# Summing the expert results in the output tensor, pass by pass, instead of gathering them at the end

## The reference: what is computed

```python
h = rmsnorm(x, odd_norm_ffn[i])
x = x + moe_swiglu(h, moe_w_router[i], moe_w_gate[i], moe_w_up[i], moe_w_down[i])

logits = xf @ w_router                       # 8 experts
top_logit, top_idx = lax.top_k(logits, 2)    # two experts for each token
gates = softmax(top_logit)
...
yb = lax.map(expert_block, (xb, block_e))    # swiglu of the rows of one expert
out = zeros.at[slot_tok].add(yb * slot_gate[:, None])
```

## Time and profile before

| | |
|---|---|
| median of three runs | 1993.7 us (1992.94 to 1994.46) |
| the profiled execution | 1992.27 us |
| its span, first to last instruction | 1990.4 us |
| PE busy | 1939.7 us (97%) |
| DVE busy / ACT busy / POOL busy | 734.7 / 651.3 / 496.7 us |
| mean DMA rate | 204 GB/s |
| mean granted clock of PE | 0.995 |

### The profile page before, as it was taken

The page is one execution under the profiler, slowest core; times in us unless marked ns, Lnnn a source line. Parts: engine busy times, 40 slices in busy tenths (PEclk is TensorE's granted clock), DMA queues, the critical chain, the costliest instruction groups (busy, mean ns, idle before and its releaser), DMA issues.

```text
span 1990.4 us, 28733 instructions
## 1 busy us (share of the span) xinstructions
PE 1939.7 (97%) x11839; PEld 1705.1 (86%) x11839; DVE 734.7 (37%) x1076; ACT 651.3 (33%) x1069; POOL 496.7 (25%) x263
## 2 busy tenths in 40 slices
PE   7999999999999999999899999999999999999996
PEld 7887778888888887877679999999999999888885
DVE  4725564210010005856632000010000101999996
ACT  4333322232222224356630000000000001888783
POOL 3546664265445543442121000000000000000010
PEclk9999999999999999999999999999999999999998
DMA  7962222233233332320009877878888787999995
GB/s 242 314 212 64 64 81 88 75 117 95 99 102 94 97 102 70 111 85 22 33 1 371 298 254 281 291 281 315 283 309 289 285 310 274 384 379 384 367 413 212
DMA packets 295103, 405.38 MB, mean 204 GB/s; under 512 B 11272, under 2 KB 211034, under 8 KB 294970
## 3 DMA queue, kind: packets, MB, share of 16 engines
q1 hardware_dynamic: 292666, 395.12, 56.9%
q0 software_dynamic: 2304, 8.39, 1.1%
HBM read 372.67 MB, written 30.80 MB: 203 GB/s over the span
## 4 chain that ended last, share of the span: by engine, by line
PE 92%; DVE 3%; POOL 2%; ACT 1%; issue 1%; DVEq 1%; SPq 0%; DMA 0%; POOLq 0%; ACTq 0%
PE ps L2000 21%; PE ps L2007 10%; PE ps L399 6%; PE ps L400 6%; PE ps L401 6%; PE ps L2061 5%; PE ps L2063 5%; PE ps L2062 5%; PE ps L417 3%; PE ps L419 3%; PE ps L418 3%; PE ps L547 2%; PE ps L549 2%; PE ps L548 2%; PE ps L436 1%; PE ps L435 1%
## 5 line engine op out<-in xcount | busy, mean ns | idle before, releaser
L1242 POOL TENSOR_TENSOR w_lo<-raw,w_hi 128x1024 fp32r<-128x1024 f32 (+1 forms) x159 | 387.9, 2448 | 353.8 <-ACT w_hi L935 353.6
L1847 DVE TENSOR_TENSOR s_lo<-s_raw,s_hi 128x1024 fp32r<-128x1024 f32 x198 | 235.4, 1222 | 22.0 <-ACT s_hi L2207 13.6
L2449 DVE TENSOR_TENSOR hid<-ps,silu_g 128x160 f32<-128x160 f32 x110 | 35.7, 324 | 543.0 <-ACT silu_g L2182 543.0
L935 ACT ACTIVATE w_hi<-raw 128x1024 fp32r<-128x1024 f32 (+1 forms) x159 | 164.8, 1043 | 192.2 <-PE ps L419 115.8
L399 PE MATMUL ps<-act_a_hi,w_hi 128*128 128x512 f32 x568 | 226.4, 399 | 0.0
L2182 ACT ACTIVATE silu_g<-ps 128x160 f32<-128x160 f32 x110 | 33.4, 304 | 585.9 <-PE ps L2000 585.9
L2000 PE MATMUL ps<-xT,w_up 128*128 128x132 f32 (+1 forms) x1760 | 224.2, 281 | 0.0
L2000 PE MATMUL ps<-xT,w_gate 128*128 128x132 f32 (+1 forms) x1760 | 224.2, 281 | 0.0
L400 PE MATMUL ps<-act_a_lo,w_hi 128*128 128x512 f32 x568 | 221.2, 390 | 0.0
L401 PE MATMUL ps<-act_a_hi,w_lo 128*128 128x512 f32 x568 | 221.2, 390 | 0.0
L2207 ACT ACTIVATE s_hi<-s_raw 128x1024 fp32r<-128x1024 f32 x198 | 205.6, 1059 | 42.6 <-PE ps L2063 37.3
(11 more groups left out here) (369 smaller groups left out, 2908.9 us busy)
## 6 DMA issues: line engine op xcount, KB each, us to landing
w_gate<-in_moe_w_gate SPq DMA_DIRECT2D x55, 1024.0 KB, 5.2
w_up<-in_moe_w_up SPq DMA_DIRECT2D x55, 1024.0 KB, 7.6
w_down<-in_moe_w_down SPq DMA_DIRECT2D x55, 1024.0 KB, 10.2
s_raw<-in_moe_w_gate SPq DMA_DIRECT2D x33, 1024.0 KB, 7.7
s_raw<-in_moe_w_up SPq DMA_DIRECT2D x33, 1024.0 KB, 7.6
s_raw<-in_moe_w_down SPq DMA_DIRECT2D x33, 1024.0 KB, 7.7
raw<-in_even_w_in SPq DMA_DIRECT2D x43, 512.0 KB, 5.2
raw<-in_attn_w_qkv SPq DMA_DIRECT2D x24, 512.0 KB, 3.7
```

The lines of the kernel that those rows point to most:

```text
L935: act.activation(w_hi[:, u % HL_SLOTS, 0:size(u)], raw[:, u % RAW_SLOTS, 0:size(u)], ACT.Copy).then_inc(hi_done, 1)
L1242: pool.tensor_tensor(w_lo[:, u % HL_SLOTS, 0:size(u)], raw[:, u % RAW_SLOTS, 0:size(u)], flat(w_hi[:, u % HL_SLOTS, 0:size(u)]), ALU.subtr ...
L1847: return eng.tensor_tensor(s_lo[u % S_HL][:], s_raw[u // 2 % S_RAW][:, u % 2, :], s_hi[u % S_HL][:].bitcast(F32), ALU.subtract)
```

## The change

The tensor `y_dram`, its zeros, the gathers and the last sums go. In their place:

- After the tile loads of round 6 of the first pass, SP stores the residual `x_sb` to `out`. From then on two of its tiles are free as `xp` and `xp2`.
- DVE computes, while the first pass begins, where each token stands in each expert's list (`tab_at`) and its token number with the gate (`tab_src`). POOL writes these pairs of 8 bytes with 32 indirect DMAs of 128 entries into a DRAM tensor `table`, sorted by pass, and SP reads it back as `tab` and `tab2` in the last round of the first pass.
- For each pass POOL fetches the rows of `out` that belong to its tokens by an indirect DMA into `xp` (and `xp2` for rows beyond 128), DVE computes `y_rows = PSUM * gate + xp` where ACT copied before, and POOL scatters `y_rows` back to `out`. Each fetch waits for the scatters of the pass before.
- In the first small pass DVE takes over the sums of the last wide pass, right behind the products of chunks 0 and 1; in the others both halves of `small_rows` are DVE's.
- After the last small pass no fetch, sum or store is left but the pass's own. The body of the extra passes (not run here) is longer.

```diff
-        zero_blocks = [(rows, r) for r in range(0, y_dram.shape[0], P) for rows in (y_dram, h_slots)]
+        zero_blocks = list(range(0, h_slots.shape[0], P))
...
@@ SP
-                if r == 1 and t >= 1:
-                    store_small_rows(t - 1)
-                if r == 2 and t == 0:
-                    store_rows(WIDE - 1)
...
-                if r == 5 and w >= 1:
-                    store_rows(w - 1)
+                if r == 6 and w == 0:
+                    sp.wait_ge(acc_evac, 44 + NT)
+                    for tt in range(NT):
+                        sp.dma_start(out[0, tt * P:(tt + 1) * P, :], x_sb[:, tt, :]).then_inc(out_stored, 16)
+                if r == ROUNDS - 1 and w == 0:
+                    by_pass = table.rearrange("(w c) a -> c w a", w=E)
+                    sp.wait_ge(scattered, 16 * 2 * NT + 16 * NT * E)
+                    sp.dma_start(tab[:], by_pass[0:P, :, :]).then_inc(tab_in, 16)
+                    sp.dma_start(tab2[0:CAP2, :, :], by_pass[P:CAP, 0:WIDE, :]).then_inc(tab_in, 16)
         for t in range(SMALL):
             load_small(t)
-        store_small_rows(SMALL - 1)
...
-        for tt in range(NT):
-            sp.wait_ge(out_made, tt + 1)
-            sp.dma_start(out[0, tt * P:(tt + 1) * P, :], x_sb[:, tt, :]).then_inc(out_stored, 16)
         sp.wait_ge(out_stored, 16 * NT)
@@ ACT
-                if r == 0 and t >= 1:
-                    small_y_copy(t - 1, 0)
...
-                if t == 0 and r == 0:
-                    act.wait_ge(y_turned, 2 * WIDE - 1)
-                    act.wait_ge(y_stored, 32 * (WIDE - 1))
-                    copy_y(y_rows, P)
...
-                if f == 4 and w >= 1:
...
-                    copy_y(y_rows, P)
@@ POOL
+        pool.wait_ge(table_ready, 1)
+        pool.wait_ge(scattered, 16 * 2 * NT)
+        for j in range(NT * E):
+            pool.indirect_dma_start(table, bass.IndirectOffsetOnAxis(ap=tab_at[:, j:j + 1], axis=0),
+                                    tab_src[:, j, :], None).then_inc(scattered, 16)
+        pool.wait_ge(tab_in, 32)
+        pool.wait_ge(out_stored, 16 * NT)
+        for w in range(WIDE):
+            m = WIDTHS[w] - P
+            if w:
+                pool.wait_ge(y_stored, 32 * w)
+            fetch(xp, tab[:, w, 0:1]).then_inc(xp_in, 16)
+            fetch(xp2[0:m, :], tab2[0:m, w, 0:1]).then_inc(xp_in, 16)
+            pool.wait_ge(y_copied, 2 * w + 1)
+            put(y_rows[:], tab[:, w, 0:1]).then_inc(y_stored, 16)
+            pool.wait_ge(y_copied, 2 * w + 2)
+            put(y_rows2[0:m, :], tab2[0:m, w, 0:1]).then_inc(y_stored, 16)
+        for t in range(SMALL):
+            if t:
+                pool.wait_ge(s_y_stored, 16 * t)
+            else:
+                pool.wait_ge(y_stored, 32 * WIDE)
+            fetch(xp, tab[:, WIDE + t, 0:1]).then_inc(xp_in, 16)
+            pool.wait_ge(s_y_copied, 2 * t + 2)
+            put(y_rows[:], tab[:, WIDE + t, 0:1]).then_inc(s_y_stored, 16)
         pool.wait_ge(s_y_stored, 16 * SMALL)
-        pool.sem_inc(pool_step, 1)
-        gather(y_higher, 1)
@@ DVE
+        other, away, first_row = steps[:, 0:32], steps[:, 32:64], steps[:, 64:72]
...
+        dve.tensor_tensor(tab_at[:], other, away, ALU.add)
...
+        dve.tensor_tensor(tab_src[:, :, 1].bitcast(F32), work[:, 0:32], work[:, 32:64], ALU.add)
+        dve.drain().then_inc(table_ready, 1)
...
+        def add_rows(w, part):
+            dve.wait_ge(y_turned, 2 * w + part + 1)
+            if w:
+                dve.wait_ge(y_stored, 32 * w)
+            dve.wait_ge(xp_in, 32 * w + 32)
+            dve.wait_ge(tab_in, 32)
+            m = (P, WIDTHS[w] - P)[part]
+            dst, g, old = ((y_rows, gates, xp), (y_rows2, gates2, xp2))[part]
+            for h in range(2):
+                cols = slice(512 * h, 512 * h + 512)
+                ins = dve.scalar_tensor_tensor(dst[0:m, cols], ps[0:m, 6 + h, :], g[0:m, w, 1:2], old[0:m, cols],
+                                               ALU.mult, ALU.add)
+            ins.then_inc(y_copied, 1)
...
+                if t == 0 and r < 2:
+                    add_rows(WIDE - 1, r)
...
-        def small_y_copy(t, h):
+        def small_rows(t):
             dve.wait_ge(s_used, (t + 1) * S_UNITS)
             dve.wait_ge(y_stored, 32 * WIDE)
             if t:
                 dve.wait_ge(s_y_stored, 16 * t)
-            dve.tensor_copy(y_rows[:, 512 * h:512 * h + 512], ps[:, h, :]).then_inc(s_y_copied, 1)
+            dve.wait_ge(xp_in, 32 * WIDE + 16 * t + 16)
+            for h in range(2):
+                cols = slice(512 * h, 512 * h + 512)
+                dve.scalar_tensor_tensor(y_rows[:, cols], ps[:, h, :], gates[:, WIDE + t, 1:2], xp[:, cols], ALU.mult,
+                                         ALU.add).then_inc(s_y_copied, 1)
...
+                if f in (4, 6) and w >= 1:
+                    add_rows(w - 1, f // 2 - 2)
...
-        for k, got in enumerate((y_lower, y_higher)):
-            for tt in range(NT):
-                j = NT * k + tt
-                dve.wait_ge(y_back[j], 16)
-                if tt == 0:
-                    dve.drain()
-                ins = dve.scalar_tensor_tensor(x_sb[:, tt, :], got[:, tt, :], gate[:, j:j + 1], x_sb[:, tt, :],
-                                               ALU.mult, ALU.add)
-                if k:
-                    ins.then_inc(out_made, 1)
```

More of the change, by code:

```diff
@@ L365, in _ @@
                     sp.wait_ge(zero_ready, 1)
[L366 to L369, removed]
+                for r in zero_blocks[u - U_XBC - 5:u - U_XBC - 4]:
+                    m = min(P, h_slots.shape[0] - r)
+                    sp.dma_start(h_slots[r:r + m, :], mix[0:m, 0:D // P, :].rearrange("p a b -> p (a b)")
+                                 ).then_inc(h_zeroed, 16)
             if u == U_A:
@@ L1738, in build_trunk, with build_experts @@
                 t_incl=t_incl, stat=stat, w_slots=w_slots, gate_in=gate_in, up_in=up_in, down_in=down_in,
[L1739 removed]
+                rt=rt, idx=idx, top_i=top_i, pass_t=pass_t, load_expert_round=load_expert_round, acc_evac=acc_evac,
+                tab_src=tab_src, tab_at=tab_at, tab=tab, tab2=tab2, token_no=token_no,
                 t_moe=(t["moe_w_gate"][0], t["moe_w_up"][0], t["moe_w_down"][0]))
[L1743 to L1744 removed]
+def build_experts(nc, out, table, h_slots, x_sb, sem, place, ps, gain, gain_in, ident, ones, t_incl, stat,
+                  w_slots, gate_in, up_in, down_in, rt, idx, top_i, pass_t, load_expert_round, acc_evac, tab_src, tab_at, tab, tab2, token_no,
                   block, h_tok, h_made, norm_h, moe_ss, scratch, t_moe):
@@ L1755, in build_experts @@
     assert o <= 5 * NT * D * 4
-    y_lower, o = place("y_lower", [P, NT, D], F32, 5 * NT * D * 4)
-    o_hid = o
+    spread, o = place("spread", [P, NT, CAP], F32, 5 * NT * D * 4)
+    spreadT, o = place("spreadT", [P, 2, SEQ], F32, o)
+    assert o <= 6 * NT * D * 4
+    o = o_hid = 6 * NT * D * 4
     hid, o = place("hid", [P, FT, CAP], F32, o)
@@ L2163, in extra_pass @@
             turn_y(P, CAP2, 3)
+            pe.wait_ge(spread_made, x + 1)
+            for tt in range(NT):
+                pe.transpose(ps[:, 0, tt * P:(tt + 1) * P], spread[:, tt, 0:P], ident[:])
+                mm = pe.transpose(ps[0:CAP2, 1, tt * P:(tt + 1) * P], spread[:, tt, P:CAP], ident[:])
+            mm.then_inc(spread_turned, 1)
+            pe.wait_ge(spread_kept, x + 1)
+            pe.wait_ge(y_copied, x * 2 + (2 * WIDE + 2))
+            for i in range(2 * NT):
+                h, ts = i // NT, slice(i % NT * P, (i % NT + 1) * P)
+                pe.matmul(ps[:, i, :], spreadT[:, 0, ts], y_rows[:, 512 * h:512 * h + 512], start=True, stop=False)
+                pe.matmul(ps[:, i, :], spreadT[0:CAP2, 1, ts], y_rows2[0:CAP2, 512 * h:512 * h + 512], start=False,
+                          stop=True).then_inc(part_done, 1)
         pe.wait_ge(extras_made, 1)
@@ L2582, in build @@
 def build(nc, t, out):
-    y_dram = nc.dram_tensor("y_rows", (MAXPASS * CAP, D), F32, kind="Internal").ap()
+    table = nc.dram_tensor("table", (E * SEQ, 2), I32, kind="Internal").ap()
     h_slots = nc.dram_tensor("h_slots", (MAXPASS * CAP, D), F32, kind="Internal").ap()
-    build_experts(nc, out, y_dram, h_slots, **build_trunk(nc, t, y_dram, h_slots))
+    build_experts(nc, out, table, h_slots, **build_trunk(nc, t, h_slots))
 def rope_table():
```

121 lines of the change are left out of this document (73 added, 48 removed).

## The result

The changed kernel takes 2009.99 us (median of four, 2008.31 to 2011.88) beside 1993.32 for the kernel before on the same chip (four, 1992.65 to 1994.46): ratio 1.0085 [1.0072, 1.0098]. It is slower by 0.85%, where 1985.8 was forecast. The profiled execution took 2010.1 us with a span of 2008.3.

The account below looks back on a forecast made before the run. PE was taken to bound the kernel (92% of the chain), with a 19.4 us tail without products. Gain 8.0 - 0.1 = 7.9 us: span 1982.5, execution 1984.4, plus 1.4 gives median 1985.8; range 1981.9 to 1990.3.

Parts of the forecast that it names:

- Hidden up to 52 ns a packet: First wide pass: table scatters at 17 ns a packet cost each DMA engine 4.4 us and stay hidden up to 52 ns.
- The forecast's room of 13.3 us: First wide pass, 1100 to 1142.6: other transfers need 29.3 of 42.6 us, leaving 13.3 us for the table.
- The third rival: First wide pass: dear 8-byte table writes slow the weight stream, PE stands up to 25 us in rounds 7 to 9, 2010; 7%.
- Tail, gain 8.0: After the last product: dropping the last gather, sums and stores ends the span at 1982.4 instead of 1990.4, gain 8.0 us.
- PE's loop is the latest of the three: Tail: of POOL's scatter, DVE's loop and PE's loop of skipped bodies, PE's ends last, draining at 1982.1.
- The forecast's own sign of an error: End of the kernel: POOL's last wait ending the span was listed among the signs that the prediction is wrong.
- Code fetch missing: Tail: PE's first skip of 3.67 us may be a one-time delay; PE drains 3.5 us sooner, gain 11.5, 1982.2; 12%.
- Small passes, 0.1: Small passes: DVE's added sums fit its spare time; PE stands only 0.1 us, at turn_hidden waiting for y_copied.
- the second rival: Small passes: all 3.8 us of DVE's added sums reach PE, gain 4.2, 1989.5; 17%.
- POOL beside DVE, 0: Small passes: POOL's seven indirect DMAs before the last product do not slow DVE's s_lo, nothing charged.
- Later wide passes, fetches and the eleven small operations, 0: Wide passes: sums hidden with 1.6 us over, fetches issued a pass ahead, DVE's 11 operations of at most 3.5 us hidden.
- Zeros, 0: Start: dropping 19 zero stores of y_dram, 9.8 MB in the first 115 us, gives nothing back, as no load was late.

Follow-up runs that it names:

- 12: Changed kernel with a table of one entry per slot, 8 scatters in place of 32, unused slots skipped by a bounds check; complete: 1985.04 us.
- run 1: Changed kernel without the 32 table scatters and the two table reads, tab filled on DVE, sums add wrong rows: 1986.67 us.
- 7: Changed kernel with only the first 8 of the 32 table scatters, table not read, sums add wrong rows: 1986.84 us.
- 13: Kernel 12 with each engine's loop over the extra passes inside one comparison that skips it whole: 1984.08 us.
- 3: Changed kernel with table entries padded from 8 to 64 bytes, still 32 scatters, complete: 2020.01 us.
- 6: Changed kernel with the 32 scatters paced four per tile of hidden units, the first sixteen going in one run: 2016.32 us.
- 4: Changed kernel with 32 scatters of 512-byte entries, table not read, sums add wrong rows: 2023.17 us.
- 8: Changed kernel with the 32 scatters replaced by 32 gathers of 8 bytes at the same addresses, sums add wrong rows: 2023.64 us.
- 10: Changed kernel with all 32 scatters in one run from the fourteenth tile on, table read in the second wide pass: 2018.78 us.
- 2: Changed kernel with the stores of out moved behind SP's table reads in the first pass's last round: 2020.51 us.
- 5: Changed kernel with the 32 scatters paced two per tile of hidden units, table read in the second wide pass: 1998.79 us.
- 9: Changed kernel with scatters from the twelfth tile, three per tile, table read in the second wide pass: 2000.37 us.

## Why the prediction was wrong

**The step that failed** is the first wide pass: "At 17 ns the table costs each engine 4.4 us ... Hidden up to 52 ns a packet." It priced the scatters by the time that their own packets take. That time was small indeed, 1.2 us of each engine in the 40 us (2.9%), less than the 4.4 forecast: the trace has 778 packets there, of some 24 ns each, where 4096 were counted for the table. It was the wrong price. While the scatters are issued, the packets of the weights take 129 ns instead of 61. The forecast's room of 13.3 us was gone, and PE stood 18.6 us and ran 5.4 us slower behind it. Without the table the time is 1986.7, with 8 scatters 1986.8, with the slot table's 8, complete, 1985.0: without the run of 32 the forecast of 1985.8 would have held. That three medians lie within about 1 us of it is partly luck: against the kernel before beside each, the gains were 4.5, 5.9 and 8.8 us, where 7.9 was forecast.

The third rival named the place and the sign (2010, PE waiting in rounds 7 to 9) at 7%. Its number is right by luck, since its reason was wrong. It asked for 83 ns or more for each 8-byte write; the writes were cheap, longer ones did not help, and gathers did the same harm. What the harmful runs have in common is many indirect DMAs in a short time.

**Point by point, by the sum.** The span was forecast at 1982.5 and was 2008.3, 25.8 more: 24.1 of the first wide pass, 1.5 of the tail, 0.25 of the small passes.

- *Tail, gain 8.0.* It was 6.5. The two sums took 1.41, not 1.28, so PE's loop began a little later, and the loop took 10.6 us, not 9.8 (a branch of 4.49 against 3.67). POOL's scatter was done at 2002.4, 7.0 after the last product, inside the bounds of 4.7 to 9.9. What was missing is POOL's own drain behind it: 5.45 us in the changed kernel, 3.49 in 12. The trace of before had one, of 8.66 us from 1977.0, and the prediction left it out. Its length goes with the number of indirect DMAs that POOL has issued: 2.84 us after 34 (run 1), 3.49 after 42 (7, 12 and 13), 5.45 after 66 (the changed kernel and every other run), 0.08 us for each. So the 32 scatters lengthen the tail, too: 12.9 us, against 11.9 in 1 and 11.8 in 7 and 12. The drain ends 0.6 us after PE in the one and 0.7 before in the other. "PE's loop is the latest of the three" held, but there was a fourth path: POOL's drain ends within 0.7 us of PE's loop, and it takes all but 1 us of what a shorter loop would give (12 and 13). DVE's loop, forecast to end 6.7 us behind the last product, was through at 2000.2, after 4.8. The forecast's own sign of an error, POOL's last wait ending the span, is what the trace shows.
- *Code fetch missing.* This rival was wrong: the long branch came back each time, 3.8 to 4.6 us, even as a single one around the whole loop.
- *Small passes, 0.1.* They took 0.35. PE waited 0.2 for `y_rows` at `turn_hidden`, and DVE's four `s_lo` behind the sums took 4.62 as before. The price of 3.8 was not paid, so the second rival fell. The other 0.15 is not accounted for.
- *POOL beside DVE, 0.* Right in sum, though the puts grew: two took 5.14 and 9.54 us where 0.97 is usual, while four of DVE's `s_lo` beside the first kept their 4.62. So the two do get in each other's way, other than the prediction read from the earlier trace rows, and here POOL bore it: the second put, from 1741.01, ended at 1750.55, 0.8 us behind eight `s_lo` in a row (1740.61 to 1749.76). The Trainium skill (SBUF — State Buffer, Who interferes with whom) says that a DVE instruction with two SBUF inputs contends with a GpSimd instruction that reads SBUF, and leaves it to the order of issue who blocks.
- *Later wide passes, fetches and the eleven small operations, 0.* Right: 122.23 us between passes in both kernels, and no wait on them.
- *Zeros, 0.* Right: from 50 to 130 us PE is busy 80.00 in both, while the DMA share fell from 0.90 to 0.67.

**What stays open.** Why a run of indirect DMAs harms at all was not shown. In the creep of 3 the data queues were idle for a while (share 0.04), so a full queue does not explain it; the one instruction fetch of 16 KB that it has between 1110 and 1140 took the usual 0.95 us, but whether an engine had waited for it to start is not seen. Nor is it shown what decides between the two forms, the slow stream and the creep; both come from the same scatters. Number, pace and scatters outstanding were varied together, so which of the three counts is open, too.

## What to carry to other kernels

Price a run of GpSimd's indirect DMAs by what else must move while it lasts, not by its own bytes: eight in a row beside a full weight stream cost PE at most 0.6 us here, since the stream had room for what they held up; thirty-two cost 24 to 37 us. So make fewer of them: one entry for each place where it is used, instead of all pairs. To let few be outstanding helps less (1996.6, against 1985.0 with eight). And when a tail is shortened, list each engine's last wait and drain, as the trace of before has them: the next path was 0.7 us behind.

## What the runs showed of the hardware

- Runs of 32 indirect DMAs, one in 1.26 us, made PE creep in five of six kernels, and a run of 16 did so in 6, mostly at one product in 1.4 to 2.8 us instead of 0.14. The first late product came 12.0 to 12.2 us behind the first DMA in 3, 4, 6, 8 and 10 (in 2 some 11), and the full row of products was back 4 to 9 us after the start of the run's last. It did so for scatters of 8, 64 and 512 bytes and for gathers, with the other queues full or idle, and for 32 x 32 transposes as for large products.
- Indirect DMAs slowed the weight stream at a DMA share of 0.8 to 1.2: to 61 GB/s at the least in the changed kernel, 149 and 165 in 5, 152 to 186 in 9, and 131 for 10 us with eight alone (7), where 1 had 398. Not always: in 3, 4 and 8 the stream kept 382 to 396 GB/s (1110 to 1120) while PE crept. For another symptom the Trainium skill (DMA: Bandwidth & Descriptors, Latency and other measured facts) guesses at contention for the ports behind which GpSimd's descriptors lie; no view here can show that.
- GpSimd's last drain, after its last DMA had landed, took 2.84, 3.49 and 5.45 us in kernels with 34, 42 and 66 indirect DMAs, whatever their size (8, 64 or 512 bytes an entry) or direction.
- PE's first branch over the long skipped body took 3.67 to 4.55 us in every kernel, the others some 0.22.
